# A transformer layer on one core: the modulation on four column tiles and mostly inside the first FFN, the first norm from token-major rows

## The chip, the cores and the metric

The kernel runs on one core of a Trainium2 chip. The metric is the time of the device for one execution, in microseconds (us), as the median of several runs. The core has a matrix engine (PE, TensorE), two elementwise engines (DVE is VectorE, ACT is ScalarE), POOL (GpSimd, hardly used here), and SP (SyncE), whose queue issues most of the DMAs. PEld is TensorE's loading of stationary data. Each engine works through its own list of instructions in order and waits at semaphores for the others.

## The reference

One layer of a diffusion transformer for 1024 latent tokens and 256 context tokens of width 1024, all in float32. A vector `c` gives, through a product with `w_mod` (1024 x 9216), nine vectors of 1024 values, and `c_ctx` the same for the context tokens:

```python
m_lat = (silu(c) @ w_mod + b_mod).reshape(1, 1, 9, 1024)
m_ctx = (silu(c_ctx) @ w_mod + b_mod).reshape(9, 1024)

def half_ffn(h, mod, i, g, w_up, w_down):
    shift, scale, gate = mod[3*i], mod[3*i + 1], mod[3*i + 2]
    n = rms_norm(h, g) * (1 + scale) + shift
    a, b = split(n @ w_up, 2)                  # w_up: 1024 x 5632
    return h + 0.5 * gate * ((silu(a) * b) @ w_down)   # w_down: 2816 x 1024
```

The layer is: `half_ffn` with i = 0 on all 1280 tokens; a norm with mod 3 and 4; one input projection `w_in` for attention, gated linear attention (GLA) and gates; both branches, merged, through `w_out`, times mod 5, added; `half_ffn` with i = 2 on the latent tokens; a last RMS norm.

## The kernel before

Most of the work keeps activations feature-major in SBUF: `h0[p, k, t]` is feature 128k + p of token t. Tokens go in chunks `ALL` = 512, 512 and 256 (`LAT` is the first two). PSUM has eight banks `ps[0..7]` of 512 fp32 columns.

A float32 weight product is made of three fp32r products (`three`, lines 190 to 194): weights and activations are each split in a high and a low part, and hi*hi, hi*lo and lo*hi are added up in PSUM. Weights arrive as *panels* of 128 x 1024 in two slots of `raw`; `load_panel` (SP) waits until the panel two earlier has been split, `split_panel` (DVE, lines 168 to 176) makes `wh` and `wl` once the last panel of that slot has been used, `wait_panel` (PE) waits for the split.

*Start.* `load_sp` issues on SP's queue: constants, small vectors, ten row blocks `x_rows` (128 tokens x 1024), then `mod_load` pieces of `w_mod`. TensorE turns each row block (`load_pe`, 8 transposes), and DVE and ACT each copy half of it to `h0` (`turn_evac`).

*Modulation.* `mod_pe` does 18 blocks of 512 columns, two halves of 4 matmuls each; the stationary is `silu_c` (128 x 2: latent and context), the moving operand 128 x 512 fp32 of `w_mod`, the result 2 x 512. `mod_copy` (DVE) takes it to `mod_row`, four narrow transposes turn it, and `mod_finish` (DVE, lines 289 to 302) adds the bias for a group of six blocks and makes `coef` and `gates`. Groups 0 and 1 run before the FFN, with the squares and sums of the first norm (`early_sums`, `early_pe`) between them; group 2 (`MOD_LATE`) runs in the GLA setup, between the decay products (line 830) and the state loop (lines 837 and 853), and its `mod_copy` calls stand between the scans on DVE.

*FFN.* `Ffn` has 11 groups; a group is four up panels (j = 0 to 3) and two down panels (j = 4, 5). Up goes panel by panel, inside over the chunks, into banks 0 to 2 (j even) and 3 to 5 (j odd); ACT makes silu, DVE `hidden` (product, high part, low part; lines 577 to 589), for panels 0 and 1 at j = 1, for 2 and 3 at j = 3. Down uses banks 6, 7, 5, and DVE adds into `h` (line 603). The groups are a loop on each engine (`run`), the last one written out. `a_free` and `b_free` begin with an increment by ACT and DVE when they reach the FFN.

```python
for j in range(6):                       # Ffn.dve, body of a group
    if j < 4:
        split_panel(dve, self.panel(g, j + 1))
    if j in (1, 3):
        hidden(g, j // 2)
```

## Time and profile before

| | us |
|---|---|
| median of 3 runs | 3167.74 |
| all runs | 3167.7, 3167.74, 3169.66 |
| the profiled execution: span | 3170.5 |
| PE busy | 2967.2 (94%) |
| DVE busy | 1561.9 (49%) |
| ACT busy | 576.2 (18%) |

The span is from the first to the last instruction of one profiled execution. The page shows each engine's busy time, then groups of instructions by line. A line such as 192 is a helper's, so many stages share it; the tiles' names tell them apart. Timelines list instructions with start and duration, and in square brackets how long the engine had been idle and what released it. A float32 matmul is recorded as two passes. The stages of this execution: rows and early modulation 0 to 115, first FFN 115 to 1026, norm and `w_in` 1027 to 1477, GLA 1477 to 1755, attention to 2166, merge and `w_out` to 2356, second FFN 2398 to 3130, last norm and output to 3170.

### The profile page before, as it was taken

The numbers are of one execution on the slowest core, as the hardware profiler recorded it, in microseconds if no ns is written. First come the engines' busy times: TensorE is split into PE (matmuls) and PEld (weight loads), VectorE is DVE, ScalarE is ACT, GpSimd is POOL, SyncE is SP. The second block draws the span as 40 slices with busy tenths as digits, with TensorE's granted clock in tenths as the row PEclk, the third lists the DMA queues.
The fourth block names the chain that finished last, engine by engine and source line by source line (L and its number), as shares of the span: only waits on it lengthen the run. The fifth ranks groups of instructions, "written<-read, shape, count | busy, mean of one in ns | idle before, by whom it ended". The sixth has DMA issues, their size and how long they took to land.

```text
span 3170.5 us, 36617 instructions
## 1 busy us (share of the span) xinstructions
PE 2967.2 (94%) x14674; PEld 2383.7 (75%) x14674; DVE 1561.9 (49%) x2541; ACT 576.2 (18%) x1023; POOL 0.2 (0%) x4
## 2 busy tenths in 40 slices
PE   8999999999999899999866779998997999999997
PEld 2588888888888588886355559997766888888885
DVE  5544444444444511111876588886535444444445
ACT  3200000000000411112311456671011000000002
POOL 0000000000000000000000000000000000000000
PEclk9999999999999899998955689999998999999999
DMA  8411111111110211232300100003411111111111
GB/s 288 146 40 40 33 39 40 40 36 37 40 40 31 76 36 50 93 98 85 120 1 1 40 1 1 1 1 106 146 33 34 46 53 46 46 46 46 48 48 57
DMA packets 188569, 175.29 MB, mean 55 GB/s; under 512 B 5774, under 2 KB 147259, under 8 KB 188347
## 3 DMA queue, kind: packets, MB, share of 16 engines
q1 hardware_dynamic: 182714, 163.50, 16.3%
q10 hardware_dynamic: 5760, 10.49, 0.9%
q8 instruction: 65, 1.06, 0.1%
q14 instruction: 30, 0.24, 0.0%
HBM read 155.10 MB, written 18.87 MB: 55 GB/s over the span
## 4 chain that ended last, share of the span: by engine, by line
PE 39%; DVE 9%; ACT 1%; issue 1%; DMA 0%; DVEq 0%; ACTq 0%
PE psum L192 9%; PE psum L194 9%; PE psum L193 9%; PE psum L1369 3%; PE psum L991 1%; PE psum L1381 1%; PE psum L1382 1%; DVE scores L1076 1%; DVE ptl L1460 1%; PE psum L1356 1%; PE psum L1357 1%; PE psum L988 1%; DVE mtot L1446 1%; PE psum L1206 1%; DVE rstd L429 0%
## 5 line engine op out<-in xcount | busy, mean ns | idle before, releaser
L192 PE MATMUL psum<-nh,wh 128*128 128x512 f32 (+2 forms) x1688 | 612.8, 363 | 0.1
L193 PE MATMUL psum<-nl,wh 128*128 128x512 f32 (+2 forms) x1688 | 612.5, 363 | 0.0
L194 PE MATMUL psum<-nh,wl 128*128 128x512 f32 (+2 forms) x1688 | 611.9, 362 | 0.0
L173 DVE CAST wh<-raw 128x1024 fp32r<-128x1024 f32 x183 | 125.7, 687 | 746.8 <-PE psum L194 724.7
L603 DVE SCALAR_TENSOR_TENSOR h<-psum,gates,h 128x512 f32<-128x512 f32 (+1 forms) x440 | 298.3, 696 | 161.4 <-PE psum L194 158.4
L192 PEld LDWEIGHTS psum<-nh,wh 128*128 128x128 f32 (+1 forms) x1688 | 317.0, 188 | 51.4
L193 PEld LDWEIGHTS psum<-nl,wh 128*128 128x128 f32 (+1 forms) x1688 | 316.9, 188 | 50.9
L194 PEld LDWEIGHTS psum<-nh,wl 128*128 128x128 f32 (+1 forms) x1688 | 316.6, 188 | 51.2
L192 PE MATMUL psum<-hidh,wh 128*128 128x512 f32 (+1 forms) x880 | 325.6, 370 | 8.4 <-DVE hidl L587 8.4
L193 PE MATMUL psum<-hidl,wh 128*128 128x512 f32 (+1 forms) x880 | 324.8, 369 | 0.0
L194 PE MATMUL psum<-hidh,wl 128*128 128x512 f32 (+1 forms) x880 | 323.8, 368 | 0.0
L192 PE MATMUL psum<-n1h,wh 128*128 128x512 f32 x704 | 274.9, 391 | 15.2 <-ACTq L562 15.2
L193 PE MATMUL psum<-n1l,wh 128*128 128x512 f32 x704 | 274.6, 390 | 0.0
L194 PE MATMUL psum<-n1h,wl 128*128 128x512 f32 x704 | 274.6, 390 | 0.0
L569 ACT ACTIVATE silu_a<-psum 128x512 f32<-128x512 f32 (+1 forms) x110 | 61.2, 556 | 1006.4 <-PE psum L194 1006.2
L582 DVE TENSOR_TENSOR prod<-silu_a,psum 128x512 f32<-128x512 f32 (+1 forms) x110 | 69.9, 635 | 334.5 <-PE psum L194 334.5
L175 DVE TENSOR_TENSOR wl<-raw,wh 128x1024 fp32r<-128x1024 f32 x183 | 223.5, 1221 | 6.3
L192 PEld LDWEIGHTS psum<-hidh,wh 128*128 128x128 f32 x880 | 165.9, 189 | 41.3 <-issue 11.9
L194 PEld LDWEIGHTS psum<-hidh,wl 128*128 128x128 f32 x880 | 165.6, 188 | 28.4
L193 PEld LDWEIGHTS psum<-hidl,wh 128*128 128x128 f32 x880 | 165.9, 189 | 27.2
L1369 PE MATMUL psum<-diag,prob 128*128 128x128 f32 x1280 | 165.5, 276 | 6.6 <-DVE ptl L1460 6.6
L1369 PEld LDWEIGHTS psum<-diag,prob 128*128 128x128 f32 x1280 | 154.9, 192 | 20.1 <-issue 18.5
(213 smaller groups left out, 3505.2 us busy)
## 6 DMA issues: line engine op xcount, KB each, us to landing
raw<-in_w_ffn_up_dram SPq DMA_DIRECT2D x88, 512.0 KB, 3.7
mod_raw<-in_w_mod_dram SPq DMA_DIRECT2D x24, 1024.0 KB, 4.9
raw<-in_w_ffn_down_dram SPq DMA_DIRECT2D x44, 512.0 KB, 3.7
raw<-in_w_in_dram SPq DMA_DIRECT2D x34, 512.0 KB, 3.7
mod_raw_late<-in_w_mod_dram SPq DMA_DIRECT2D x12, 1024.0 KB, 5.1
gates_saved<-staged ACTq DMA_DIRECT2D x40, 256.0 KB, 2.0
merge_gate<-gates_saved SPq DMA_DIRECT2D x8, 1024.0 KB, 5.1
x_rows<-in_x_dram SPq DMA_DIRECT2D x8, 512.0 KB, 7.4
```

Source lines behind the costliest of these rows:

```text
L173: nc.vector.tensor_copy(wh[:, par, 0:n], raw[:, par, 0:n]).then_inc(panel_split, 1)
L175: nc.vector.tensor_tensor(wl[:, par, 0:n], raw[:, par, 0:n], wh[:, par, 0:n].bitcast(F32), ALU.subtract).then_inc(panel_split, 1)
L192: pe.matmul(o, hi_w, hi_x, start=first, stop=False)
L193: pe.matmul(o, hi_w, lo_x, start=False, stop=False)
L194: return pe.matmul(o, lo_w, hi_x, start=False, stop=last)
L569: nc.scalar.activation(silu_a[:, c, 0:w], ps[c][:, 0:w], ACT.Silu).then_inc(self.a_free, 1)
L582: nc.vector.tensor_tensor(prod[:, c % 2, 0:w], silu_a[:, c, 0:w], ps[3 + c][:, 0:w], ALU.mult).then_inc(self.b_free, 1)
L603: nc.vector.scalar_tensor_tensor(hk, down, gates[:, self.gate_i, k, s:s + 1], hk, ALU.mult, ALU.add).then_inc(self.down_free, 1)
L988: pe.matmul(o, vtok[:, ch, hd * DV:(hd + 1) * DV], scores[:, par, cc, t, :], start=True, stop=False)
L991: mm = pe.matmul(o, states[r, d, ch, t, :], qdec[r, d, t, cc * P:(cc + 1) * P], start=False, stop=(d == 1))
L1076: nc.vector.copy_predicated(dst, m, src).then_inc(g_pred, 1)
L1369: mm = pe.matmul(turned_of(i, r)[:, (kt - a) * P:(kt - a + 1) * P], probs[i % 3][:, kt * P:(kt + 1) * P], diag[:, i % 2, :], start=True, s ...
```

## The change

- The modulation is cut in nine *sections* (one vector of 1024 each, two blocks). The 4 matmuls of a half go to four column tiles: `silu_c` is padded with zeros to 32 columns, and matmul j writes partitions 32j to 32j+31 of bank 6 or 7. `mod_copy` copies all 128 partitions; `mod_turn` turns and adds the four tiles' rows in one step with 8 matmuls against a selection matrix `K_SEL` (128 x 2) into bank 6; `mod_finish` follows for each section.
- Sections 0 and 1 are done before the FFN (ring of three buffers as before). Sections 2 to 8 are done in groups 0 to 6 of the first FFN, from a ring of one buffer: halves behind steps 2, 3, 5 and 6 of the twelve up products, the turn behind step 9. Down waits for `mod_evac`. The late group in the GLA setup is gone.
- The x rows are loaded by ACT's queue. ACT squares and sums each row block token-major (`accum_out`), takes the root, DVE inverts and scales the rows, and TensorE turns rows twice: unscaled to `h0`, scaled to `xr`. `FirstNorm` then applies scale and shift only: ACT makes the high part, DVE the full value and the low part.
- `Ffn.run` is written out for all groups of both FFNs. In group 0 the up products go by chunk within a pair of panels (`order`). The first panel is loaded and split ahead of the FFN.

```diff
+    def mod_load(sp, s, h):
+        p = 4 * s + h
+        if s < MOD_EARLY:
+            if p >= 3:
+                sp.wait_ge(mod_product, p - 2)
+            sp.dma_start(mod_slot(s, h)[:, :, :], mod_src(s, h)).then_inc(mod_loaded[p % 3], 16)
+        else:
+            sp.wait_ge(mod_product, p)
+            if p == 4 * MOD_EARLY:
+                sp.wait_ge(n0_lo, N0_UNITS)
+            sp.dma_start(mod_slot(s, h)[:, :, :], mod_src(s, h)).then_inc(ring_loaded, 16)
+    def mod_half(pe, s, h):
...
+        if s >= 1 and h == 0:
+            pe.wait_ge(mod_evac, s)
+        if s >= 1 and h == 2:
+            pe.wait_ge(mod_copied, 2 * s)
+        bank = ps[6 + h // 2]
+        for j in range(4):
+            mm = pe.matmul(bank[32 * j:32 * j + 32, :], silu_c[:, 4 * (h % 2) + j, :], mod_slot(s, h)[:, j, :],
+                           start=(h % 2 == 0), stop=(h % 2 == 1))
+        mm.then_inc(mod_product, 1)
+    def mod_turn(pe, s):
+        for b in range(2):
+            pe.wait_ge(mod_copied, 2 * s + b + 1)
+            for q in range(4):
+                m = 4 * b + q
+                mm = pe.matmul(ps[6][:, 2 * m:2 * m + 2], mod_row[:, b, q * P:(q + 1) * P], cst[:, K_SEL, 0:2],
+                               start=True, stop=True)
+        mm.then_inc(mod_turned, 1)
...
+        for s in range(MOD_EARLY):
+            for h in range(4):
+                if (s, h) == (MOD_EARLY - 1, 2):
+                    ffn0.load_up(sp, 0, 0)
+                mod_load(sp, s, h)
...
+        for n, (i, scaled) in enumerate(turns):
+            if scaled:
+                turn_evac(copy, n, i, 1, 1, turn_evac_s)
+                continue
+            act.wait_ge(rows_loaded[i], 16)
+            nc.scalar.activation(x_junk[:, :], x_rows[:, i, :], ACT.Square,
+                                 accum_out=x_ss[:, i:i + 1]).then_inc(x_sq, 1)
+            act.wait_ge(x_sq, i + 1)
+            nc.scalar.activation(x_inv[:, i:i + 1], x_ss[:, i:i + 1], ACT.Sqrt, bias=eps, scale=1.0 / D)\
+                .then_inc(x_root, 1)
+            turn_evac(copy, n, i, 1, 0, turn_evac_s)
+        act.wait_ge(cols_copied, 4)
+        nc.scalar.activation(silu_c[:, :, 0], cols_a[:, A_C:A_C + 8], ACT.Silu).then_inc(silu_c_done, 1)
...
+        def dve(self, dve):            # FirstNorm
+            def full(u):
...
+                nc.vector.tensor_scalar(xn[:, u % 3, 0:w], xr[:, k, t0:t0 + w], coef[:, 0, k, s:s + 1],
+                                        modv[:, k, s:s + 1], ALU.mult, ALU.add).then_inc(n0_full, 1)
+            full(0)
+            for u in range(N0_UNITS):
+                if u + 1 < N0_UNITS:
+                    full(u + 1)
...
+                dve.wait_ge(n0_hi, u + 1)
+                nc.vector.tensor_tensor(nl0[:, k, t0:t0 + w], xn[:, u % 3, 0:w], nh0[:, k, t0:t0 + w].bitcast(F32),
+                                        ALU.subtract).then_inc(n0_lo, 1)
...
+        def order(self, g):
+            js = [(0, 1), (2, 3)] if g == 0 else [(0,), (1,), (2,), (3,)]
+            return [(j, c) for pair in js for c in range(len(self.chunks)) for j in pair]
...
             def body(g, last):         # Ffn.sp
+                mod = self.sections[g] if g < len(self.sections) else None
                 for j in range(4):
+                    if mod is not None and j in (0, 3):
+                        mod_load(sp, mod, j // 3)
+                    if not (g == 0 and j == 0 and self.first_loaded):
+                        self.load_up(sp, g, j)
                 for j in range(4, 6):
+                    if mod is not None:
+                        mod_load(sp, mod, j - 2)
...
+                    if mod is not None and n in MOD_SLOTS:
+                        if n == MOD_SLOTS[0]:
                             pe.wait_ge(self.down_free, g * (8 * C) + self.n_down)
+                        mod_half(pe, mod, MOD_SLOTS.index(n))
+                    if mod is not None and n == MOD_TURN_SLOT:
+                        mod_turn(pe, mod)
+                if mod is not None:
+                    pe.wait_ge(mod_evac, mod + 1)
                 for j in range(4, 6):
...
                     if j < 4:          # Ffn.dve
                         split_panel(dve, self.panel(g, j + 1))
+                    if mod is not None and j in (1, 2):
+                        mod_copy(dve, mod, j - 1)
                     if j in (1, 3):
                         hidden(g, j // 2)
+                    if mod is not None and j == 3:
+                        mod_finish(dve, mod)
...
         load_dve(dve)
+        for s in range(MOD_EARLY):
+            if s == MOD_EARLY - 1:
+                split_panel(dve, pn(PANEL0))
+            for b in range(2):
+                mod_copy(dve, s, b)
+            mod_finish(dve, s)
+        norm0.dve(dve)
         ffn0.dve(dve)
```

## Rows read from the trace of the kernel before

**Rows 1.** The page: busy time and share per engine; two groups, busy and mean ns.

```profile
PE 2967.2 (94%) x14674; PEld 2383.7 (75%) x14674; DVE 1561.9 (49%) x2541; ACT 576.2 (18%) x1023; POOL 0.2 (0%) x4
...
L173 DVE CAST wh<-raw 128x1024 fp32r<-128x1024 f32 x183 | 125.7, 687 | 746.8 <-PE psum L194 724.7
...
L175 DVE TENSOR_TENSOR wl<-raw,wh 128x1024 fp32r<-128x1024 f32 x183 | 223.5, 1221 | 6.3
```

**Rows 2.** Groups of instructions, 0 to 125 us: count, busy us, mean ns, idle before.

```profile
L274 PE MATMUL psum<-mod_raw,silu_c 128*2 128x512 f32 x192 | 83.9, 592 | 1.7 <-DMA mod_raw<-in_w_mod_dram 1.7
...
L317 ACT ACTIVATE h<-psum 128x512 f32<-128x512 f32 x10 | 6.0, 597 | 8.8 <-PE psum L251 8.8
```

**Rows 3.** Timeline of PE at the FFN's start: start us, duration us, instruction.

```profile
115.46 0.49 PE L192 MATMUL psum<-nh,wh 128*128 128x512 f32 x1
115.79 0.40 PE L193 MATMUL psum<-nl,wh 128*128 128x512 f32 x1
116.02 0.39 PE L194 MATMUL psum<-nh,wl 128*128 128x512 f32 x1
```

**Rows 4.** Timeline of PE, end of up and begin of down in group 0.

```profile
170.55 0.28 PE L194 MATMUL psum<-nh,wl 128*128 128x256 f32 x1
170.67 0.40 PE L192 MATMUL psum<-hidh,wh 128*128 128x512 f32 x1
```

**Rows 5.** Timeline of DVE at the same place, the last chunk's last hidden step.

```profile
171.74 0.43 DVE L587 TENSOR_TENSOR hidl<-prod,hidh 128x256 fp32r<-128x256 f32 x1
```

**Rows 6.** Timeline of PE in the state loop; x8 are eight passes.

```profile
1566.47 0.66 PE L853 MATMUL psum<-vtok,ktok 128*64 128x128 f32 x8 [0.48 <-ACT ktok L883]
1567.07 0.44 PE L837 MATMUL psum<-cst,la 128*128 128x128 f32 x2
```

**Rows 7.** Timeline of PE, the sums of the qk norms.

```profile
1772.72 18.08 PE L1206 MATMUL psum<-cst,qk_sq 128*128 128x2 f32 x84 [6.41 <-ACT qk_sq L1177]
```

**Rows 8.** Windows: PE, PEld, DVE, ACT, POOL busy (count), PEclk, DMA share, GB/s.

```profile
1780.00:1790.00 10.00, 10.00 (x48) 10.00 (x49) 9.59 (x17) 4.43 (x6) 0.00 (x0) 0.50 0.00 0
2397.60:2401.00 3.40, 3.40 (x8) 2.72 (x9) 3.13 (x4) 1.92 (x2) 0.00 (x0) 0.50 0.01 2
2402.00:2403.00 1.00, 1.00 (x6) 0.82 (x5) 0.00 (x0) 0.00 (x0) 0.00 (x0) 1.00 0.72 196
```

**Rows 9.** DMA of 0 to 50 us: GB/s in 40 slices; issues, median us to landing.

```profile
GB/s 0 113 347 175 17 328 397 233 377 410 413 419 419 419 416 405 387 387 387 390 383 385 152 221 405 256 300 400 179 352 382 154 400 310 13 262 401 211 334 403
...
mod_raw<-in_w_mod_dram SPq DMA_DIRECT2D x9, 1024.0 KB, 4.9
```

**Rows 10.** Timelines of the SP queue and of DVE around the first panel.

```profile
103.13 0.37 SPq L212 DMA_DIRECT2D mod_raw<-in_w_mod_dram  x1
103.89 14.81 SPq L184 DMA_DIRECT2D raw<-in_w_ffn_up_dram  x4
...
110.09 0.69 DVE L173 CAST wh<-raw 128x1024 fp32r<-128x1024 f32 x1 [4.62 <-DMA raw<-in_w_ffn_up_dram]
```

**Rows 11.** Timelines of DVE and PE in the GLA setup.

```profile
1530.10 3.26 DVE L905 TENSOR_TENSOR_SCAN cum<-cst,la 128x128 f32<-128x128 f32 x10
1535.06 0.68 DVE L287 COPY mod_row<-psum 2x512 f32<-2x512 f32 x1 [1.70 <-PE psum L264]
...
1544.78 2.91 DVE L915 TENSOR_TENSOR la<-dexp,gk_f 128x1280 f32<-128x1280 f32 x2
...
1550.72 0.81 PE L837 MATMUL psum<-cst,la 128*128 128x128 f32 x4
```

**Rows 12.** Timelines of DVE and ACT behind the state loop: 1024- and 512-wide steps.

```profile
1580.07 0.69 DVE L1029 TENSOR_SCALAR qc<-gq_f 128x1024 f32<-128x1024 f32 x1
1580.68 0.69 DVE L1047 TENSOR_TENSOR eq_b<-cum 128x512 f32<-128x512 f32 x1
1581.28 0.69 DVE L1048 TENSOR_TENSOR eq_b<-cum 128x512 f32<-128x512 f32 x1
...
1583.20 1.06 ACT L1008 ACTIVATE eq_b<-eq_b 128x1024 f32<-128x1024 f32 x1 [5.81 <-DVE ek_b L1050]
```

More of the change, by code:

```diff
@@ L304, in turn_evac, with turn @@
-    def turn_evac(nc_copy, q, done):
-        for i in range(TOK // P):
-            u = 2 * i + q
-            nc_copy(u, h0[:, 4 * q:4 * q + 4, i * P:(i + 1) * P],
-                    ps[u % 6][:, :].rearrange("p (k t) -> p k t", k=4)).then_inc(done, 1)
+        def turn(n, i, q, scaled):
+            u = 2 * n + q
+            if u >= 6:
+                pe.wait_ge(turn_evac_s if q else turn_evac_v, (u - 6) // 2 + 1)
+            for k in range(4):
+                row = slice((4 * q + k) * P, (4 * q + k + 1) * P)
+                src = xs_rows[:, i % 2, row] if scaled else x_rows[:, i, row]
+                mm = pe.transpose(ps[u % 6][:, k * P:(k + 1) * P], src, ident)
+            mm.then_inc(turned, 1)
@@ L310, in load_act, with turn_evac @@
+        pe.wait_ge(silu_c_done, 2)
+        for s in range(MOD_EARLY):
+            if s == 0:
+                pe.wait_ge(cols_copied, 4)
+            for h in range(4):
+                mod_half(pe, s, h)
+            mod_turn(pe, s)
+    def turn_evac(nc_copy, n, i, q, scaled, done):
+        u = 2 * n + q
+        dst = xr if scaled else h0
+        nc_copy(u, dst[:, 4 * q:4 * q + 4, i * P:(i + 1) * P],
+                ps[u % 6][:, :].rearrange("p (k t) -> p k t", k=4)).then_inc(done, 1)
     def load_act(act):
-        act.wait_ge(cols_copied, 3)
@@ L376, in high @@
                                      bias=modv[:, 8 * 3 * self.i + k, s:s + 1]).then_inc(self.hi_done, 1)
-            if early:
-                for c in range(C):
-                    for k in range(KT):
-                        square(c, k)
-                    root(c)
-            else:
-                for k in range(KT):
-                    square(0, k)
+            for k in range(KT):
+                square(0, k)
             for c in range(C):
-                if not early:
-                    root(c)
+                root(c)
                 for k in range(KT):
@@ L391, in act @@
                         high(c, k)
-                    if c + 1 < C and not early:
+                    if c + 1 < C:
                         square(c + 1, k)
@@ new lines, in body @@
+                    t0, w = self.chunks[c]
+                    if c == 0:
+                        wait_panel(pe, self.panel(g, j))
+                    if j == 0:
+                        self.norm.normed(pe, c)
+                    pe.wait_ge(self.b_free if half else self.a_free, g * (2 * C) + (t * C + c + 1))
+                    if j == 1 and c == 2:
+                        pe.wait_ge(self.down_free, g * (8 * C) + self.n_down)
+                    o = ps[c + 3 * half][:, 0:w]
+                    for k in range(KT):
+                        mm = three(pe, o, wh[:, self.slot(j), k * P:(k + 1) * P],
+                                   wl[:, self.slot(j), k * P:(k + 1) * P],
+                                   self.norm.hi[:, k, t0:t0 + w], self.norm.lo[:, k, t0:t0 + w],
+                                   k == 0, k == KT - 1)
@@ L555, in wait_up @@
             if c < C - 1:
-                eng.wait_ge(self.up_done, g * (4 * (C - 1)) + ((2 * t + half) * (C - 1) + c + 1))
+                place = [jc for jc in self.order(g) if jc[1] < C - 1].index((2 * t + half, c))
+                eng.wait_ge(self.up_done, g * (4 * (C - 1)) + place + 1)
             else:
@@ L926, in gla_state_dve @@
         decayed_keys(3)
-        for n in range(2 * MOD_GROUP + 4, MOD_BLOCKS):
-            mod_copy(dve, n)
-        mod_finish(dve, 2)
         dve.wait_ge(g_elast, 1)
```

310 lines of the change are left out of this document (138 added, 172 removed).

## The prediction

> **What bounds the kernel now.** I read the page first: TensorE is busy 94% of the span, VectorE 49% and ScalarE 18% [rows 1], so a microsecond of TensorE work or of TensorE waiting is nearly a microsecond of the result, except where the chain of waits runs elsewhere. Then the timelines of the three places that the change touches.
>
> *Start.* The input rows are turned by 22 us; from there the 12 early blocks of the modulation keep TensorE. The groups of instructions show 192 records of it, 83.9 us [rows 2]: 96 fp32 matmuls of two passes, 0.43 us a pass, 3.44 us for four of them. The FFN's first product starts at 115.46 [rows 3], at full clock.
>
> *First FFN.* Its products follow each other without a gap, 0.23 us for 512 columns [rows 3] and 0.12 for 256. Also from the last up product of a group to the first down product there is none: 170.55 to 170.67 [rows 4], since down begins on a chunk whose hidden values are long ready, while VectorE does the last chunk until 172.17 [rows 5].
>
> *GLA setup.* The last six blocks run beside scans and exponentials of VectorE and ScalarE, and hold up the state loop only a little [rows 11].
>
> **The change, part by part.** All is reckoned as a difference, so the profiled execution's own span, 3170.5, gives the terms, and the sum is set on the median of the runs, 3167.7; the two differ by 0.1%.
>
> *Rows at the start.* The x loads go to ScalarE's queue, and each row now costs ScalarE a Square over 1024 (1.06, as the 1024-wide Exp [rows 12]), a root (0.2), two 512-wide copies instead of one (0.60 each, about 0.5 from start to start [rows 2]) and a wait for its own square: about 2.5 us. Ten rows from about 6 us on (ten DMA issues stand first on that queue) end near 31; the last scaled row is turned near 33, then a table load (1.28) and the two silus: 34 to 35. VectorE (two copies, one 0.69 scaling: 2.1 us a row) and TensorE are below that. Bytes are no limit here: cst, rows and the first three mod loads are 9.1 MB, 23 us at 390 to 419 GB/s [rows 9].
>
> *Sections 0 and 1.* Eight half products, but only three of their loads fit ahead; five more of 1 MB and the FFN's first panel follow once the first slot is free, at about 36. They are bound by DMA: 2 us to begin, 5.8 MB at 390 GB/s [rows 9], 14.8 us: the last lands at 53, whatever the tiles do, as long as a half product is under 2.7 us. Product, copy, turn and the two small VectorE steps: coef_done at about 56.8 (bounds 52 and 61).
>
> *First norm.* VectorE has two instructions a unit: a tensor_scalar (0.69 for 1024 columns [rows 12], so about 0.4 for 512) and a subtraction at 0.60 from start to start [rows 12]: 1.0 us a unit, 16 units, and 0.6 for the 8 narrow ones, 21 us; done at 77.8. Before, the norm's VectorE steps took 33 us beside the mod work.
>
> *Panel 1.* Here the gain is partly given back. Group 0 goes by chunk, so its second product is (panel 1, chunk 0). But SP issues section 2's first load ahead of panel 1's, and that load waits for all 24 n0_lo. So panel 1 is issued at 78 behind 1 MB. The same pair of loads stood there before: issued at 103.13 and 103.89, and VectorE could start the split at 110.09 [rows 10], 6.9 us after the first. Then cast and subtraction, 0.687 and 1.221 [rows 1]: TensorE gets its second product at 86.8. It has done one (5.5 us) by then, so this equals a start at 81.4: **34.1 us earlier** (bounds 29 and 39). Unlike before, TensorE comes out of a long idle time; after such a time the FFN of the second half ran its first 4.4 us at half clock [rows 8], which costs **2.2 us**.
>
> *Seven sections inside the FFN.* Each is 16 fp32 matmuls, which TensorE can't overlap with the FFN's own, since these use the whole array. One after another they would be 13.7 us. Two column tiles side by side are shown by the state products (64 columns wide, in two column halves, 128 columns streamed): eight passes from 1566.47 to the next instruction at 1567.07 [rows 6], 0.60 us, where 0.107 a pass one after another would be 0.856. Two tiles at once would be 0.43, so 0.17 is paid once a burst. Four at once I price the same way: 0.86 + 0.17 = 1.03 us a half, 4.1 a section. The trace doesn't show four; the bounds are 0.86 and, if no more than two run together, 1.72 + 0.17 = 1.89 a half. Turn: 8 real matmuls of 128x128 weights by 2 columns replace narrow transposes. The same shape stands in the qk norms: 84 passes in 18.08 us at half clock [rows 7, 8], so 0.107 at full clock; 16 passes, 1.7 us, 1.8 with the switch.
>
> The Trainium skill speaks against full gain from four tiles (TensorE: Matmul & The Clock Gate, Part 3): it reports 3.07 times for four row tiles at 512 columns and 2.38 times for three column tiles; TensorEngine Tiling (Array Packing), Key Properties, adds that a change of tiling mode drains the engine. By 3.07 a half would be an estimated 1.12 us instead of 0.86, and with the 0.17 the whole some 7 us slower than my sum. The 0.17 above is what the trace shows of such a drain.
>
> *The new wait before down.* Ahead of down TensorE now waits for mod_evac, because banks 6 and 7 are lent to the modulation. mod_finish stands on VectorE behind the last chunk's hidden steps: they end at 172.17 [rows 5], the small add takes 0.21, TensorE goes on at about 172.6 instead of 170.67 [rows 4]: **1.95 us in each of seven groups**, where nothing waited before. Queued behind the wait on TensorE are the down products, and behind those everything. In group 0 it is worse: by chunk, panel 2 is free only after the last product but one, VectorE splits panel 4 (1.95) before any hidden step, and then has three chunks to do (about 1.8, 1.8, 1.2): down starts 4.2 us after the last up product, 2.3 more.
>
> A section is thus 4.1 + 1.8 + 1.95 = 7.9; seven and the 2.3 make **57.6 us more**. The ring load for the next half is issued when the last half is done and lands in 4.9 us [rows 9], while TensorE has a 5.46 us product to do: just covered, 0.5 to spare; if the cover fails it is a few tenths at two places a section, 0 to 4 us in all. VectorE's two 0.67 copies and the other SP waits fall where there is slack of microseconds. Loops written out: the products of w_in are written out now and run gapless, so I take 0. FFN 1 by chunk: its start waits for ScalarE to leave the norm, as before; 0.
>
> *GLA setup without modulation.* VectorE loses three copies (0.58 each with their place in the queue) and one with 1.70 of waiting [rows 11]: 4.0 us, so the last decayed keys end at 1543.7 instead of 1547.7, and TensorE turns the first keys at once rather than at 1550.72 [rows 11]: **6.9 us earlier**, less 0.3 as TensorE is at half clock there; 6.6 gained. What is late next is VectorE's own chain.
>
> **Sum.** -34.1 + 2.2 + 57.6 - 6.6 = +19.1. On 3167.7: **3187 us**.
>
> **The rivals.**
> *Two at a time* (streams of four tiles don't all fit): for it, the trace has no four, and all shown rates are at most two fp32 streams. Section 11.3, seven 79 + 2.3, start unchanged: +43, **3211**. Chance 0.17.
> *The tiles don't run together at all*, the change not doing what it says: half 3.5, section 18, seven 126 + 2.3; the start becomes TensorE-bound, 7 us later: +95, **3263**. Against it are the 0.60 us of [rows 6]. Chance 0.06.
> *Other side: the input phase runs at the DMA's best rate.* Place: before the FFN. 14.9 MB at 419 GB/s [rows 9] are 36 us; were the rows no chain on ScalarE and the last mod load there at 38 instead of 53, the equal of a start would be 66 instead of 81.4, and the time 3172 with sections as priced, **3162** with sections at their lower bound of 6.6. It decides for faster from a start before 56, or before 65 with that section. Against it is the order: silu stands behind all rows on ScalarE, and only three loads go ahead. Chance of under 3161: 0.06; of ending within 0.2%: 0.09.
> My case, four tiles and the waits as priced: 0.62.
>
> **How the numbers follow.** Measurement of this kernel tells from no change what is over about 0.2%, 6.3 us. Bounds of my own case: start 39 and section 6.6 (halves of 0.86, turn 1.2, wait as is) give +5, 3172; start 29 earlier with the DMA cover failing by 4 gives +28. To hold 8 in 10 the range takes in two at a time: 3172 to 3214. Faster 0.06, same 0.10, slower 0.84.
>
> **What would show it.** First FFN product near 72 and second near 87, with TensorE idle between and panel 1's DMA as releaser; a burst of mod matmuls of 1.0 us (1.9: two at a time; 3.5: none); a wait of 2 us for modv before down in seven groups, 4 in the first; the end of FFN 0 some 25 us later than 1026; first key turn some 7 us closer to the end of w_in. Wrong if the wait for mod_evac is short, if a burst costs well under 0.9, or if the start is before 65.

## The result and the profile after

Before: 3168.69 us median (3167.7 to 3169.66, 4 runs). After: 3202.79 us (3202.32 to 3204.96, 4 runs). The ratio is 1.0111 with a 95% interval of [1.0098, 1.0123]: the change makes the kernel 1.1% slower. The profiled execution of the changed kernel spans 3201.0 us against 3170.5. In the changed kernel the three products of `three` are L199 to L201, the split of a panel is L180 and L182, a half product of the modulation is L242 and its turn L252.

The page, first engine lines (busy us, share of the span, instructions), against [rows 1]:

```profile
PE 2911.0 (91%) x14820; PEld 2387.9 (75%) x14820; DVE 1546.4 (48%) x2551; ACT 556.1 (17%) x1018; POOL 0.2 (0%) x4
```

TensorE is busy 91% instead of 94%: 56 us less busy time in 30 us more span. To see where, I took the same four marks in both traces: the last down product of the first FFN, VectorE's memset that opens the GLA setup, ScalarE's first decayed query behind the state loop, and the end.

| stretch | before | after | difference |
|---|---|---|---|
| start and first FFN | 1026.5 | 1068.2 | +41.7 |
| norm 1 and w_in | 451.6 | 453.0 | +1.4 |
| GLA setup and states | 97.3 | 89.9 | -7.4 |
| rest | 1595.1 | 1589.9 | -5.2 |

In the rest the change touches only the second FFN: its loops are written out, and its group 0 goes by chunk. From its first up product to the end of its last down product it takes 730.1 us instead of 732.1. At the first down product of each group TensorE waits a little less, here in group 0, before and after:

```profile
2445.59 0.49 PE L192 MATMUL psum<-hidh,wh 128*128 128x512 f32 x1 [0.77 <-DVE hidl L587]
2476.68 0.50 PE L199 MATMUL psum<-hidh,wh 128*128 128x512 f32 x1 [0.61 <-DVE hidl L688]
```

Below, `e_tiles` keeps the loops and takes 732.1, and `j_panels` has them written out without the order by chunk and takes 730.4: so 2.0 of the 5.2 us come with the loops written out. The other 3.2 lie ahead of the second FFN (4.2 less) and behind it (1.0 more). Across all the kernels below the whole rest lay between 1587.5 and 1595.1 us, and apart from those 2.0 it follows no edit. So I judge edits by the first three stretches of the profiled execution, and by the medians second.

*The start.* The timeline of PE (start us, us, instruction, count, idle time before and what ended it), against [rows 3]:

```profile
61.69 3.58 PE L252 MATMUL psum<-cst,mod_row 128*128 128x2 f32 x16
74.92 0.77 PE L199 MATMUL psum<-nh,wh 128*128 128x512 f32 x1 [9.66 <-DVE nl L441]
...
97.28 0.80 PE L199 MATMUL psum<-nh,wh 128*128 128x512 f32 x1 [15.28 <-DVE wl L182]
...
110.47 1.06 PE L242 MATMUL psum<-mod_ring,silu_c 128*32 128x512 f32 x8
111.46 0.50 PE L199 MATMUL psum<-nh,wh 128*128 128x512 f32 x1
```

The first product starts at 74.92, when VectorE has the first token chunk of the norm. Then TensorE stands for 15.3 us until panel 1 is split. SyncE's and VectorE's timelines show why, against [rows 10]:

```profile
88.19 0.37 SPq L227 DMA_DIRECT2D mod_ring<-in_w_mod_dram  x1
88.61 1.13 SPq L191 DMA_DIRECT2D raw<-in_w_ffn_up_dram  x2
```

```profile
65.52 0.17 DVE L271 SCALAR_TENSOR_TENSOR coef<-modv,cols_a 128x16 f32<-128x16 f32 x1
...
95.27 0.69 DVE L180 CAST wh<-raw 128x1024 fp32r<-128x1024 f32 x1 [7.17 <-DMA raw<-in_w_ffn_up_dram]
```

The ring load is issued at 88.19, when the norm ends, panel 1 behind it, and VectorE can cast it 7.1 us after the first of them. What kept the norm late is coef at 65.5. The transfer rates of 0 to 62 us, in 40 slices of 1.55 us, against [rows 9]:

```profile
GB/s 0 148 375 396 409 396 400 399 402 402 403 400 407 399 382 391 268 5 0 0 0 0 0 0 0 0 24 242 410 328 382 395 374 321 383 385 384 103 7 0
```

From 28.3 to 41.6 us the transfer engines stand, 13 us: three loads fill the slots, and the fourth waits for a half product that waits for the silus behind all ten rows on ScalarE.

*The sections.* In the FFN a burst of four matmuls (eight passes) takes 1.00 us, 110.47 to 111.46 above; the turn:

```profile
148.41 1.84 PE L252 MATMUL psum<-cst,mod_row 128*128 128x2 f32 x16
150.11 0.37 PE L199 MATMUL psum<-nh,wh 128*128 128x256 f32 x1
```

A group without a section takes 82.8 us from up to up, one with a section 91.2 (280.85 to 372.02): 8.4 us. The view of the waits of PE from 60 to 800 us (total, times, longest):

```profile
PE psum L199 <- DVE wl L182: 15.3, 1, 15.3
PE psum L199 <- DVE modv L266: 12.3, 7, 4.0
PE psum L199 <- DVE nl L441: 9.7, 1, 9.7
PE psum L242 <- DMA mod_raw<-in_w_mod_dram: 2.3, 1, 2.3
PE psum L242 <- DMA mod_ring<-in_w_mod_dram: 0.3, 1, 0.3
```

Behind the two waits of the start stand seven waits for modv ahead of down, the longest 4.0 in group 0 and the others 1.4, and practically none for the ring's loads. Behind the 4.0 us wait TensorE also falls to the lower clock level. Windows of that place (PE, PEld, DVE, ACT, POOL busy, granted clock, DMA share, GB/s), against [rows 8]:

```profile
155.00:159.00 4.00, 1.11 (x10) 0.91 (x8) 3.86 (x8) 0.00 (x0) 0.00 (x0) 1.00 0.45 131
160.00:162.00 2.00, 1.88 (x5) 1.50 (x6) 0.24 (x2) 0.00 (x0) 0.00 (x0) 0.50 0.00 0
162.00:164.00 2.00, 2.00 (x8) 1.64 (x7) 0.75 (x1) 0.00 (x0) 0.00 (x0) 0.72 0.00 0
164.00:168.00 4.00, 4.00 (x23) 3.41 (x22) 3.39 (x5) 0.00 (x0) 0.00 (x0) 1.00 0.01 2
```

Before the wait it had 1.00, behind it 0.50 and then 0.72, and group 0's down products take 29.2 us instead of 27.7.

*GLA setup.* The first keys are turned as soon as VectorE's last decayed keys are there, after 40 us without work for TensorE, against [rows 11]:

```profile
1586.22 1.09 PE L939 MATMUL psum<-cst,la 128*128 128x128 f32 x4 [40.30 <-DVE la L1014]
```

### The profile page after: what moved, and what is told of

Its sections match the earlier page's. It is cut to its first block and busy times, and to the rows that moved or that the text cites. A ratio compares the mean times of both kernels' runs of the same rounds, so it can differ in the third digit from the quotient of the medians.

```text
span 3201.0 us, 35078 instructions
## 1 busy us (share of the span) xinstructions
PE 2911.0 (91%) x14820; PEld 2387.9 (75%) x14820; DVE 1546.4 (48%) x2551; ACT 556.1 (17%) x1018; POOL 0.2 (0%) x4
## 5 line engine op out<-in xcount | busy, mean ns | idle before, releaser
L199 PE MATMUL psum<-nh,wh 128*128 128x512 f32 (+2 forms) x1688 | 619.3, 367 | 24.9 <-DVE wl L182 15.3
L201 PE MATMUL psum<-nh,wl 128*128 128x512 f32 (+2 forms) x1688 | 614.1, 364 | 0.0
L180 DVE CAST wh<-raw 128x1024 fp32r<-128x1024 f32 x183 | 125.6, 686 | 772.7 <-PE psum L201 747.2
L199 PEld LDWEIGHTS psum<-nh,wh 128*128 128x128 f32 (+1 forms) x1688 | 318.1, 188 | 99.9 <-issue 23.1
L201 PEld LDWEIGHTS psum<-nh,wl 128*128 128x128 f32 (+1 forms) x1688 | 317.6, 188 | 52.2
L199 PE MATMUL psum<-hidh,wh 128*128 128x512 f32 (+1 forms) x880 | 327.1, 372 | 19.0 <-DVE modv L266 12.3
L201 PE MATMUL psum<-hidh,wl 128*128 128x512 f32 (+1 forms) x880 | 324.3, 368 | 0.0
L199 PE MATMUL psum<-n1h,wh 128*128 128x512 f32 x704 | 274.7, 390 | 15.2 <-ACTq L663 15.2
L201 PE MATMUL psum<-n1h,wl 128*128 128x512 f32 x704 | 274.5, 390 | 0.0
L182 DVE TENSOR_TENSOR wl<-raw,wh 128x1024 fp32r<-128x1024 f32 x183 | 223.4, 1221 | 6.3
L199 PEld LDWEIGHTS psum<-hidh,wh 128*128 128x128 f32 x880 | 166.2, 189 | 53.4 <-DVE modv L266 13.7
L201 PEld LDWEIGHTS psum<-hidh,wl 128*128 128x128 f32 x880 | 165.9, 189 | 28.5
```

Source lines behind the costliest of these rows:

```text
L180: nc.vector.tensor_copy(wh[:, par, 0:n], raw[:, par, 0:n]).then_inc(panel_split, 1)
L182: nc.vector.tensor_tensor(wl[:, par, 0:n], raw[:, par, 0:n], wh[:, par, 0:n].bitcast(F32), ALU.subtract).then_inc(panel_split, 1)
L199: pe.matmul(o, hi_w, hi_x, start=first, stop=False)
L201: return pe.matmul(o, lo_w, hi_x, start=False, stop=last)
```

## The experiments

All edits are on the changed kernel, except for `e_tiles`. "End" is the end of the first FFN (changed kernel 1068.2), ratios are to the kernel before, run beside on the same chip; the changed kernel's is 1.0111. Where an edit leaves the start alone, the first product's start still moves between 72.5 and 75.5 us from kernel to kernel, with the time of the last early half product (58.2 to 60.4 us, behind a wait of 0.6 to 3.0 us for its load) and the clock of the turn behind it (1.95 us in `d_gla`, 3.57 or 3.58 in the changed kernel, `a_panel1`, `b_split`, `b_credits`, `c_finish`, `d_gla2` and `j_panels`), so an end is good to about 2 us; where this matters the start is given beside it.

### Do four column tiles run at the same time? `g_two` and `g_one`

```diff
-            mm = pe.matmul(bank[32 * j:32 * j + 32, :], silu_c[:, 4 * (h % 2) + j, :], ...
-                           start=(h % 2 == 0), stop=(h % 2 == 1))
+            r = 32 * (j % 2)          # g_one: r = 0
+            mm = pe.matmul(bank[r:r + 32, :], silu_c[:, 4 * (h % 2) + j, :], ...
+                           start=(h % 2 == 0 and j < 2), stop=(h % 2 == 1 and j >= 2))   # g_one: j < 1, j >= 3
```

The copies and the turn take the 64 or 32 rows that are in use.

> Edit on the changed kernel: a half product uses two column tiles, two matmuls after each other on each, instead of four. Theory (matmuls on different tiles run at the same time, each at the 0.86 us of two passes of 512): a half takes 1.72 and what stands at its edges instead of 0.86, 0.86 more, 28 times in the FFN: 24 us more, 3227; the early sections stay behind their loads. Rival (no more than two ran together in the changed kernel): no change, 3203.

> Edit on the changed kernel: a half product as four matmuls after each other on one column tile. Theory: 3.44 us and its edges instead of 0.86, 2.58 more in each of 28 halves, 72 us, and the start 5 to 7 later since a half is then longer than a load: 3280. Rival (part of the matmul is no stream, and what overlapped was only that): well under this, 3220 to 3250.

Measured: 3234.41 us, ratio 1.0214 [1.0197, 1.0231], and 3289.18 us, 1.0383 [1.0365, 1.04]. The first burst inside the FFN in each, with the product behind it:

```profile
111.03 1.91 PE L243 MATMUL psum<-mod_ring,silu_c 128*32 128x512 f32 x8
112.87 0.50 PE L199 MATMUL psum<-nh,wh 128*128 128x512 f32 x1
```

```profile
116.20 3.62 PE L243 MATMUL psum<-mod_ring,silu_c 128*32 128x512 f32 x8
119.75 0.50 PE L199 MATMUL psum<-nh,wh 128*128 128x512 f32 x1
```

From burst to product: 3.55 us on one tile, 1.84 on two, 1.00 on four [rows 3 for the products around them]. That is 0.43 us a pass times 8, 4 and 2, and 0.11 to 0.14 on top. The tiles run together fully; what the burst pays is a constant, and my 0.17 from [rows 6] was near it. All 28 bursts in the FFN take these times in each of the three kernels. The rival "two at a time" is out. `g_one` started its first product at 81.3, 6.3 later, since a half product is then longer than a load takes.

Both came out above the forecast: by the medians 31.6 and 86.4 us more than the changed kernel where I had 24 and 77, by the end of the FFN 29.3 and 85.0. The bursts account for 23.5 and 71.4 of it, the start for 0.3 and 6.4, and a slower turn (1.87 us with 64 or 32 rows in use, 1.70 with 128) for 1.2. Most of what is left is the clock, which in two groups of `g_two` and three of `g_one` fell right behind a turn, with no wait ahead of it:

```profile
438.41 1.94 PE L253 MATMUL psum<-cst,mod_row 64*128 64x2 f32 x16
```

```profile
438.40:440.30 1.90, 1.90 (x18) 1.88 (x17) 1.72 (x3) 0.00 (x0) 0.00 (x0) 1.00 0.01 2
440.60:444.00 3.40, 3.40 (x9) 2.64 (x8) 0.00 (x0) 0.00 (x0) 0.00 (x0) 0.50 0.00 0
```

Such a group takes 96.5 us from up to up in `g_two` instead of 94.9.

### What does the place of mod_finish cost? `c_finish`

```diff
+                    chunked = g == 0 and mod is not None and j == 3
+                    if chunked:
+                        hidden(g, 1, (0, 1))
+                        mod_finish(dve, mod)
                     if j < 4:
                         split_panel(dve, self.panel(g, j + 1))
...
-                    if j in (1, 3):
+                    if mod is not None and j == 3 and not chunked:
+                        mod_finish(dve, mod)
+                    if chunked:
+                        hidden(g, 1, (2,))
+                    elif j in (1, 3):
                         hidden(g, j // 2)
                     if mod is not None and j == 3:
-                        mod_finish(dve, mod)
```

In group 0, where VectorE splits panel 4 late, the order is: hidden values of chunks 0 and 1, `mod_finish`, split, hidden values of chunk 2.

> Edit on the changed kernel: VectorE does mod_finish ahead of the last chunk's hidden values (in group 0: hidden values of chunks 0 and 1, mod_finish, split of panel 4, hidden values of chunk 2). Theory (TensorE's wait ahead of down is only the place of mod_finish in VectorE's order): the seven waits of 12.3 us in all go, and with the first one the half clock of group 0's down products (1.5): 13.8 us less, 3189. Rival (down then waits for panel 4's split or the hidden values, which were just as late): 4 us less or nothing, 3199 to 3203.

Measured: 3188.69 us, 1.0064 [1.0047, 1.0081]; the end at 1053.5, 14.7 earlier, 1.0 of it from the first product. The same waits as above:

```profile
PE psum L199 <- DVE wl L182: 14.9, 1, 14.9
PE psum L199 <- DVE nl L441: 9.7, 1, 9.7
PE psum L242 <- DMA mod_ring<-in_w_mod_dram: 1.8, 3, 0.9
```

The line on modv is gone and nothing took its place but 1.5 us more of waiting for the ring's loads. Group 0's down products take 27.7 us again instead of 29.2, so the half clock went with the wait. A group with a section now takes 89.5 us (274.08 to 363.60): a section is 6.7, of which 4.0 are half products, 1.7 the turn, and 1.0 remains for five returns to the FFN's products. These 0.2 each were not in my sum.

### What holds the second product? `a_panel1`, `b_split`, `b_credits`

`a_panel1` lets SyncE issue panel 1 ahead of the ring load:

```diff
+                ahead = g == 0 and self.first_loaded
+                if ahead:
+                    self.load_up(sp, 0, 1)
                 for j in range(4):
                     if mod is not None and j in (0, 3):
                         mod_load(sp, mod, j // 3)
-                    if not (g == 0 and j == 0 and self.first_loaded):
+                    if not (ahead and j < 2):
                         self.load_up(sp, g, j)
```

> Edit on the changed kernel: in group 0 SyncE issues the load of panel 1 ahead of section 2's first ring load, which waits for the whole first norm. Theory (panel 1 is late because it stands behind the ring load): the second product starts about 90.1 (norm ends at 88.1, split 1.95) instead of 97.3, so 7.2 us less, 3195.6. Rival (the transfer is hidden or something else, such as the ring load that is now later, becomes late): less than 2 us of change, 3201 to 3203.

Measured: 3199.25 us, 1.0089 [1.0072, 1.0106]. The second product starts at 90.40, 6.9 earlier, the end is 1062.9, 5.3 earlier (1.1 went into waits for the ring's loads, which are now the late ones). By the medians it is 3.5 us less, by the ratios 7, and their intervals overlap. The theory of the place stands, since the second product moved by 6.9 of the 7.2 us; the gain at the FFN's end was below it.

`b_split` also has the split ahead, inside the norm:

```diff
+        ffn0.load_up(sp, 0, 1)            # behind the last early mod_load
...
                                         ALU.subtract).then_inc(n0_lo, 1)
+                if u == KT - 1:
+                    split_panel(dve, pn(PANEL0 + 1))
```

and the ring load's wait for `n0_lo` is taken out (its buffer is free by then).

> Edit on the changed kernel: panel 1 is loaded right behind the last early modulation load and split by VectorE after the first token chunk of the norm; the ring load no longer waits for the norm. Theory (TensorE has work from chunk 0 on, and only panel 1 keeps it from it): the FFN runs on from 74.9 without a gap, which equals a start 17 us earlier: 3184 to 3187. Rival (TensorE then waits for the norm of chunks 1 and 2, 10.4 us a chunk on VectorE with the split, so that part of it comes back): 7 to 12 us less, 3191 to 3196.

Measured: 3200.79 us, 1.0103 [1.0086, 1.012], the end at 1062.6. Neither theory nor rival. The timelines of VectorE and PE:

```profile
76.05 1.23 DVE L182 TENSOR_TENSOR wl<-raw,wh 128x1024 fp32r<-128x1024 f32 x1
```

```profile
75.51 0.77 PE L199 MATMUL psum<-nh,wh 128*128 128x512 f32 x1 [9.66 <-DVE nl L440]
...
90.10 0.77 PE L199 MATMUL psum<-nh,wh 128*128 128x512 f32 x1 [7.29 <-DVEq L677]
```

The panel was split at 77.2, chunk 1 of the norm is not asked for yet, and TensorE stood until 90.1, released by VectorE's queue. The second product writes the other half's banks and waits for `b_free`, and its first credits are given by a `sem_inc` at the head of VectorE's FFN program, that is, behind the norm. The trace of the changed kernel could not show this wait, because there the panel came later than the credit. `b_credits` moves only these two instructions:

```diff
+        ffn0.credits(dve)      # sem_inc of b_free and down_free, until now first in ffn0.dve
         norm0.dve(dve)
         ffn0.dve(dve)
```

> Edit on b_split: VectorE gives out the first credits for the second product's banks (b_free, down_free) ahead of the first norm instead of behind it. In b_split TensorE still stood from 82.8 to 90.1, released by VectorE's queue and not by the panel, whose split had ended at 77.2. Theory (that credit is the wait that b_split ran into): TensorE goes on at 82.7 without a gap, 7.4 us and 2.2 of half clock less than b_split, the FFN's end 14 to 16 us before that of the changed kernel (1068.2): near 1053, and 3186 to 3191. Rival (TensorE then waits for the norm of chunk 1 and 2): the FFN's end at 1058 or later.

Measured: 3187.62 us, 1.0069 [1.0053, 1.0084], the end at 1049.6, 13.0 before that of `b_split` and 18.6 before the changed kernel's. TensorE has no gap of its own from 73.34 up to 112 us. So the start had three waits, one behind the other: the panel behind the ring load, VectorE's split behind the norm, and the credit behind the norm. The first alone gives 5.3 us at the end, the first two 5.6, all three 18.6. The median of 3187.62 is of four runs from 3181.57 to 3194.34, the widest spread of any kernel here, and the profile is of the shortest of them.

### What is the order by chunk worth? `j_panels`

```diff
-            js = [(0, 1), (2, 3)] if g == 0 else [(0,), (1,), (2,), (3,)]
+            js = [(0,), (1,), (2,), (3,)]
```

> Edit on the changed kernel: group 0 of the first FFN goes panel by panel like the others, no longer chunk by chunk. Theory (the order by chunk asks for panel 1 after one product, and panel 1 and VectorE's credits are there only behind the norm, while panel 0's products of chunks 1 and 2 could fill that time): 8.2 us of products move into the gap between 82 and 97, the wait ahead of down shrinks from 4.0 to 1.7 and the half clock behind it goes: the end of the FFN 8 to 12 us before 1068.2, 3191 to 3195. Rival (the order by chunk is what lets TensorE use the norm early, as it is meant to): the end of the FFN at 1066 or later, 3200 or more.

Measured: 3190.27 us, 1.0071 [1.0054, 1.0087], the end at 1055.1, 13.1 earlier. The edit also takes the order by chunk out of the second FFN, which takes 730.4 us with the edit and 730.1 without it, so the difference comes from the first. The old order does panel 0's products of chunks 1 and 2 where the new one stands:

```profile
74.44 0.77 PE L199 MATMUL psum<-nh,wh 128*128 128x512 f32 x1 [9.65 <-DVE nl L441]
...
92.96 1.07 PE L242 MATMUL psum<-mod_ring,silu_c 128*32 128x512 f32 x8 [1.62 <-issue]
96.72 0.50 PE L199 MATMUL psum<-nh,wh 128*128 128x512 f32 x1 [2.70 <-DVE wl L182]
```

The order by chunk costs 12 to 13 us as it stands; with the panel and the credits in time (`b_credits`) it ends 5.5 before the old order (4.4 without the difference of the starts). The old order with the panel and the credits in time was not run, so what the order by chunk is worth then stays open.

### Is the start bound by the silus? `s_silu`

```diff
                                  accum_out=x_ss[:, i:i + 1]).then_inc(x_sq, 1)
+            if i == 0:
+                act.wait_ge(cols_copied, 4)
+                ... the two Silu activations, until now behind all rows ...
...
+            if n in MOD_TURNS:             # TensorE, among the row turns; MOD_TURNS = [13, 15, 17]
...
+                mod_half(pe, 0, MOD_TURNS.index(n))
```

> Edit on the changed kernel: the two silus of c stand behind ScalarE's first Square instead of behind all ten rows, and TensorE does the first three half products between the row turns. Theory (the loads of sections 0 and 1 wait for slots, since the first half product waits for the silus behind the rows; the transfer engines idle from 26 to 39 us): loads go on from about 26, coef_done comes at 46 to 50 instead of 65.7, and the whole start moves by 16 to 19 us: 3184 to 3187. Rival (the start is bound by the bytes or by ScalarE's rows, which the two more table loads make 3 us longer): under 6 us less, 3197 or more.

Measured: 3193.81 us, 1.0083 [1.0066, 1.01]; the first product at 65.76, 9.2 earlier, the end at 1060.1. The rates, in the same slices as above:

```profile
GB/s 0 145 403 394 411 384 402 405 399 403 402 398 402 406 389 383 242 7 0 0 25 284 400 333 349 366 378 319 378 390 391 124 9 0 0 0 0 0 0 0
```

The gap of the transfers shrank from 13 to about 4 us and coef came at 56.4 instead of 65.5. The mechanism holds, but the gain was half of the forecast. The first half product runs at 30 us, at its turn; that it stands so late is not the reason, since in `h_all2` below it runs at 27.3 and the first product of the FFN still starts at 66.49. In both the fourth half product stands behind all the row turns, at 39.0 and 39.2, and SyncE issues the last two early loads, which need its slot and the next, only from 40.2 and 40.4 on. Even so the second product starts at 88.16, the equal of a start at 82.7, far from the 66 that the rival of the other side reckoned with: behind coef stand VectorE's norm of 22 us and panel 1, 9.2 us.

### Is a section cheaper in the GLA setup? `d_gla`, `d_gla2`

Sections 6 to 8 leave the FFN. Their half products stand among and behind the decay logits, with three slots:

```diff
+        for m in range(MOD_GLA, MOD_SECTIONS):      # TensorE, d_gla2: all behind the logits
+            for h in range(4):
+                mod_half(pe, m, h)
+            mod_turn(pe, m)
         pe.wait_ge(g_kk, 4)
```

> Edit on the changed kernel: sections 6, 7 and 8 go back to the GLA setup, four column tiles as in the FFN, their half products between and behind the decay logits, copies of two sections on VectorE ahead of its scans and of the third on ScalarE. Theory (a section costs 8.4 us inside the FFN and nothing in a place where TensorE idles for 40 us): 25 us less in the FFN and the setup at 95 to 97 us: 3178 to 3180. Rival (what the modulation costs in the setup is its copies and its transfers, not its matmuls, so that the setup goes back to the 102.7 of before or above it): 17 less or a smaller gain, 3186 or more.

Measured: 3193.41 us, 1.0076 [1.006, 1.0093]. The end is 27.0 earlier, 2.4 of it from the first product, so 24.6 for three sections; the setup takes 105.6 instead of 89.9. VectorE's timeline:

```profile
1534.67 0.69 DVE L281 COPY mod_row_late<-psum 128x512 f32<-128x512 f32 x1 [3.85 <-PE psum L260]
1539.72 0.69 DVE L281 COPY mod_row_late<-psum 128x512 f32<-128x512 f32 x1 [4.35 <-PE psum L260]
1543.21 0.18 DVE L287 TENSOR_TENSOR modv<-psum,cols_a 128x16 f32<-128x16 f32 x1 [2.81 <-PE psum L270]
...
1543.52 1.49 DVE L1038 TENSOR_TENSOR la<-cum,la 128x1280 f32<-128x1280 f32 x1
```

ScalarE had the first Ln at 1534.2; VectorE's la stands behind copies and a finish that wait for TensorE, and starts at 1543.5. I had put the copies where VectorE was idle, but they wait themselves, and what stands behind them in VectorE's list waits with them.

> Edit on d_gla, whose GLA setup took 105.6 us to the first decayed query instead of 89.9 (scans held back by 9 us by VectorE's second pair of copies, decay logits by the half products between them, which ran at half clock): all half products behind the logits, only section 6's copies on VectorE, the other four on ScalarE behind its last Ln, turns on banks of their own so that no half product waits for a mod_finish. Theory (the modulation costs the setup only what stands in the chain of logits, Ln, scans): setup back to 90 to 93 us, the end of the FFN 26 to 27 earlier as in d_gla: 3175 to 3180. Rival (transfers, or ScalarE's place, hold it): setup over 97, 3184 or more.

Measured: 3183.93 us, 1.0051 [1.0036, 1.0067]; setup 95.4, the end at 1044.8. Two waits are left in VectorE's order, of 1.5 and 2.8 us:

```profile
1547.45 0.17 DVE L292 TENSOR_TENSOR modv<-psum,cols_a 128x16 f32<-128x16 f32 x1 [1.53 <-PE psum L275]
...
1558.71 1.49 DVE L1058 TENSOR_TENSOR la<-dexp,gk_f 128x1280 f32<-128x1280 f32 x1 [2.81 <-ACT dexp L1017]
```

The second is for ScalarE, whose last copy waited for the last load. So a section costs 8.4 us in the FFN (6.7 with `c_finish`) and about 1.8 in the setup.

### The tiles alone: `e_tiles`

On the kernel before, all in its old place: the same tile matmuls, copies of 128 rows, and turns that sum the tiles.

```diff
-                    mm = pe.matmul(ps[6 + n % 2][0:2, :], silu_c[:, 4 * half + k, :], mod_slot(p)[:, k, :],
-                                   start=(p % 2 == 0 and k == 0), stop=(p % 2 == 1 and k == 3))
+                    mm = pe.matmul(ps[6 + n % 2][32 * k:32 * k + 32, :], silu_c[:, 4 * half + k, :],
+                                   mod_slot(p)[:, k, :], start=(p % 2 == 0), stop=(p % 2 == 1))
```

> Edit on the kernel before: only the four column tiles (a half product as four matmuls on four tiles, the turn as matmuls that sum the tiles), everything in its old place: twelve blocks ahead of the FFN, six in the GLA setup. Theory (the early modulation was bound by TensorE and is then bound by its 24 MB of loads, 2.7 us each, so that the last lands near 81 and VectorE's norm ends near 90): the first FFN starts at about 92 instead of 115.5, the setup gains 0 to 3: 3142 to 3146. Rival (the copies and the norm on VectorE, 33 us behind block 5, set the start all the same, or the loads with three slots come slower than 3.5 us each): start at 105 or later, 3158 or more.

Measured: 3160.54 us, 0.9976 [0.9966, 0.9985]. The FFN starts at 104.20 instead of 115.46, at half clock, and ends 8.6 earlier. The rival is nearer: from 28 to 84 us TensorE waits for loads eight times, 12.0 us in all, and at the end for VectorE's copies, which stand inside and behind the norm:

```profile
96.62 1.05 PE L266 MATMUL psum<-cst,mod_row 128*128 128x2 f32 x8
100.77 3.57 PE L266 MATMUL psum<-cst,mod_row 128*128 128x2 f32 x16 [3.10 <-DVE mod_row L289]
104.20 0.77 PE L194 MATMUL psum<-nh,wh 128*128 128x512 f32 x1
```

The setup takes 97.2 us as before (97.3) though its bursts are shorter: it is not the length of the matmuls that the setup pays for. There TensorE waits 6.3 and 5.0 us for VectorE's `mod_row` copies, which stand between the scans. So the column tiles alone make the kernel before faster by 0.2%, and the rest of the change turns this into 1.1% slower.

### Together: `h_all2`

`b_credits`, `c_finish`, `d_gla2` and `s_silu` (its half products at turns 11, 13 and 15) in one kernel.

> All together on the changed kernel: b_credits, c_finish, d_gla2, and s_silu with the three half products at turns 11, 13 and 15. Theory (the terms are in different places and add up: start 15 and 10, finish 14, sections 26): 62 to 66 us below the changed kernel, 3137 to 3141, and so about 1% below the kernel before. Rival (they overlap: with an earlier start TensorE waits for the norm's later chunks, and fewer sections leave fewer waits to take away; overlap of 8 to 12): 3146 to 3153.

Measured: 3147.82 us (3146.06 to 3151.86, 5 runs), 0.9938 [0.9924, 0.9951]: 0.6% faster than the kernel before, 1.7% than the changed one. The end is 1007.7, 60.5 earlier, where the four alone sum to 64.8; the setup takes 95.7. The parts add up but for 4 us, and the median lies in the rival's range because the setup's 6 us, which I had left out of the forecast, come on top: the rival's overlap of 8 to 12 did not come. PE's waits:

```profile
PE psum L202 <- DVE nl L474: 9.7, 1, 9.7
PE psum L260 <- DMA mod_ring<-in_w_mod_dram: 1.4, 2, 1.0
```

Of waits, little is left in the FFN's stretch but that for the norm's first chunk. The first product starts at 66.49 and the others follow without a gap up to 106 us.

## Why the prediction was right or wrong

I forecast 3187 us in a range of 3172 to 3214 and measured 3202.8: slower, as said, but 34.1 us by the medians instead of 19.1. The mechanisms named were right; sizes were off, nearly all on the same side, and one wait of the start was not seen. That the time lies in the range is in part luck: the bounds of my own case ended at +28, 3196 us, and the range went on to 3214 only to take in two tiles at a time, which `g_two` refutes. The start's bounds (29 to 39 us earlier, coef between 52 and 61) were both missed, with 23.6 and 65.7, and the first FFN ended 41.7 us later, not 25.

| term | forecast | profile |
|---|---|---|
| start, as the equal of one without a gap | -34.1 | -23.6 |
| half clock behind the gap | +2.2 | +2.3 |
| seven sections | 7 x 7.9 = +55.3 | 7 x 8.4 and a remainder of 0.4: +59.1 |
| group 0: longer wait, and half clock behind it | +2.3 | +2.3 and +1.5 |
| norm 1 and w_in | 0 | +1.4 |
| GLA setup | -6.6 | -7.4 |
| rest | 0 | -5.2, of it -2.0 from the loops written out |
| sum | +19.1 | +30.4 |

*The start is the step that failed in size*, by 10.5 us. (The second product at 97.28 less one product of 5.46 equals a start at 91.8, against 115.46.) Four places in it: ScalarE had its first row at 7.1 instead of 6 and paid two table loads of 1.28 among the rows, so that the silus ended at 38.5 instead of 35. The last early load landed at 59.8 instead of 53: the transfers began again at 41.6 instead of 38, and ran at about 370 GB/s with a slow first 3 us. The last half product, turn and finish took 5.9 us instead of 3.8, since the granted clock was 0.50 there (59.8 to 65.3): the turn alone took 3.58 instead of 1.8. Not every wait for a load had this behind it: the burst at 56.43, behind a wait of 2.4 us, still ran in 1.1 us, at 1.00 (56.4 to 57.3). In the kernel before the clock was 1.00 all the way from 20 to 115 us, with TensorE at work nearly without a gap; in the changed kernel it was 0.67 on average from 36.9 to 115. I had charged the half clock to the FFN and not to the phase ahead of it. The norm took 22.3 instead of 21. The last term, panel 1 behind the ring load, was right: 9.2 us from the end of the norm to the second product, forecast 9.0; `a_panel1` took away 6.9 of them. What I did not see there is that the credit for the second product's banks stands behind the norm on VectorE too, as the split does, so that no order of the loads could bring the second product ahead of 90 (`b_split`, `b_credits`).

*The four tiles* were priced right, 1.03 against 1.00, and `g_two` and `g_one` show it to be for the reason given, except that the prediction called its 0.17 a drain: [rows 6] show 0.60 us for eight passes, and the 0.17 is what a subtraction leaves. Weighed against the trace, the Trainium skill's 3.07 for four row tiles (TensorE: Matmul & The Clock Gate, Part 3) is below what four column tiles did here, 3.55 to 1.00. TensorEngine Tiling (Array Packing), Key Properties, says that a change of tiling mode drains the engine; the 0.11 to 0.14 on each burst fits that, but no run here separates a drain from other costs at the edges.

*The wait ahead of down* was placed right (seven, the longest in group 0, for modv) and `c_finish` shows its whole price: 13.7 us at the end of the FFN without the difference of the starts, with 1.65 in a plain group where I had 1.95. In group 0 it was 4.0, forecast 4.2; the half clock behind it was not in the sum, though the same effect was at the FFN's start.

*The cover of the ring loads* held: 0.3 us in all. *The GLA setup* gave 7.4 for 6.6. *The rival of the other side*, an input phase at the best rate of the transfers, was rightly small for this kernel: with only the silus early the equal of a start is 82.7, and it wanted 66. But what kept the kernel from it was the order of instructions and not the bytes, for `h_all2`, with the silus, the panel, its split and the credit ahead, starts at 66.5 without a gap.

*The loops written out* I took at 0. In the first FFN that holds (82.8 us for a group without a section in both), in the second they gave 2.0 us. *Norm 1 and w_in*, 0 in the sum, took 1.4 more: behind the norm the clock was 0.50 from 1098.4 to 1115.4 us, 17.0 us, where before it was 0.50 from 1057.1 to 1070.7, 13.6 us. 3.4 us more at half clock are an estimated 1.7 of work lost; no edit was made on it.

What stays open is the rest of the kernel without the 2.0 us, 3.2 us shorter in the profile after with the same instructions. The granted clock in it differs without an edit: in the first three stretches of 100 us behind the state loop it was 0.54, 0.60 and 0.67 in the profile before and 0.62, 0.62 and 0.71 in the one after. TensorE's work is the same in both and no run here tells what sets the clock there.

## What to carry over

When an edit lets an engine start early, list every wait of its second instruction too, not only the first's: here panel, split and an initial `sem_inc` (the credit that opens a buffer) each stood behind the same norm, and only with all three moved ahead did the end of the FFN come 18.6 us earlier. Work put into a full engine's stretch costs its own length and each return, 6.7 to 8.4 us a section here; in a stretch where the engine idles it costs only what its helpers' waits do to the chain, so put there the copies that never wait. And a helper's result needed at a stage's start belongs ahead of the last step of the previous stage in that helper's list.

## What was not expected of the hardware

Behind a wait of only 4.0 us TensorE ran its next 2 us at half clock (0.50, then 0.72), while the six waits of 1.4 us left it at full clock. A wait is not needed for it: in `g_two` and `g_one` the clock fell to 0.50 for over 3 us right behind a turn, in the midst of work without a gap, in two and three of the groups, and no run here tells why in these. Four fp32 column tiles of 32 columns ran at 3.55 times the speed of one, with 0.14 us on top of two passes, but each return to the FFN's products cost another 0.2. And ahead of the FFN, where TensorE works in short bursts between loads, the turn of a section cost 3.58 us at a clock of 0.50 instead of 1.84 at 1.00.
